# One matmul for the spread, mask first, values together, a shorter first selection and an earlier projection in a two-block kernel

## The reference

```python
score = sum_h w[t,h] * relu(qi[t,h] . ki[s] / sqrt(32))         # index score, masked to s <= t
idx = top_k(score, 256)
p = softmax(q . k[idx] / 8 + bias); o = p @ v[idx]              # DSA
p = softmax(q . k / 8 + c[t] - c[s], s <= t); o = p @ v         # FOX, c = cumsum log f
out = (o * silu(z)) @ w_out
```

## Time and profile before

| what | value |
|---|---|
| median of 3 runs | 3086.24 us (3084.36 to 3088.47) |
| profiled execution | 3079.65 us |
| its span | 3077.8 us, 40092 instructions |
| TensorE busy | 2876.6 us, 93% |
| VectorE busy | 1143.6 us, 37% |
| ScalarE busy | 895.2 us, 29% |
| GpSimd busy | 1031.6 us, 34% |

### The profile page before, as it was taken

One profiled execution on the slowest core, in us unless ns is written; L12 is line 12 of the kernel. 1 busy time (PEld: TensorE's weight loads), 2 busy tenths in 40 slices (PEclk: granted clock), 3 DMA queues, 4 the chain that ended last, 5 costly groups with the idle time before them and its releaser, 6 DMA issues.

```text
span 3077.8 us, 40092 instructions
## 1 busy us (share of the span) xinstructions
PE 2876.6 (93%) x16604; PEld 2199.7 (71%) x16604; DVE 1143.6 (37%) x2460; ACT 895.2 (29%) x1689; POOL 1031.6 (34%) x447
## 2 busy tenths in 40 slices
PE   6979977989899999999999999999999999998998
PEld 4746665668666666666787778787777878786886
DVE  7999987456522222223334201111111111114322
ACT  4412312452333333334212222222222222223112
POOL 2522273124322222123543333333333333333541
PEclk8979989999999999999999999999999999999999
DMA  4100011031111111112112111111111111113211
GB/s 102 35 21 21 21 53 54 29 111 42 42 48 42 49 49 42 48 49 76 55 59 78 41 42 42 42 42 42 39 45 35 48 42 42 42 42 131 62 48 62
DMA packets 222369, 155.05 MB, mean 50 GB/s; under 512 B 26294, under 2 KB 209116, under 8 KB 222060
## 3 DMA queue, kind: packets, MB, share of 16 engines
q1 hardware_dynamic: 210220, 122.62, 13.8%
q10 hardware_dynamic: 11968, 29.87, 2.7%
HBM read 132.99 MB, written 19.47 MB: 50 GB/s over the span
## 4 chain that ended last, share of the span: by engine, by line
PE 82%; DVE 8%; issue 3%; ACT 3%; POOL 2%; DMA 1%; ACTq 0%; DVEq 0%; POOLq 0%
PE proj L883 21%; PE proj L885 20%; PE proj L884 20%; PE score L1158 3%; PE out L1193 3%; PE score L1178 3%; DVE arena L2202 2%; DVE arena L2200 2%; PE score L1311 1%; PE out L1364 1%; PE out L1369 1%; PE out L1204 1%; PE score L1341 1%; PE out L883 1%; PE out L885 1%
## 5 line engine op out<-in xcount | busy, mean ns | idle before, releaser
L883 PE MATMUL proj<-act_hi,w_hi 128*128 128x512 f32 x2592 | 1056.7, 408 | 51.7 <-POOL w_lo L758 25.2
L756 POOL TENSOR_TENSOR w_hi<-w_raw,ones 128x1024 fp32r<-128x1024 f32 x181 | 431.7, 2385 | 1794.1 <-PE proj L885 1774.2
L884 PE MATMUL proj<-act_lo,w_hi 128*128 128x512 f32 x2592 | 1023.0, 395 | 0.0
L885 PE MATMUL proj<-act_hi,w_lo 128*128 128x512 f32 x2592 | 1022.8, 395 | 0.0
L883 PEld LDWEIGHTS proj<-act_hi,w_hi 128*128 128x128 f32 x2592 | 495.4, 191 | 185.2 <-issue 43.0
L885 PEld LDWEIGHTS proj<-act_hi,w_lo 128*128 128x128 f32 x2592 | 494.2, 191 | 107.8
L884 PEld LDWEIGHTS proj<-act_lo,w_hi 128*128 128x128 f32 x2592 | 495.9, 191 | 97.0 <-issue 0.2
L758 POOL TENSOR_TENSOR w_lo<-w_raw,w_hi 128x1024 fp32r<-128x1024 f32 x181 | 447.5, 2472 | 14.2
L1764 ACT ACTIVATE arena<-proj 128x512 f32<-128x512 f32 x236 | 174.9, 751 | 722.2 <-PE proj L885 696.5
L2340 DVE SCALAR_TENSOR_TENSOR arena<-arena,score 128x256 f32<-128x256 f32 (+1 forms) x192 | 76.9, 428 | 771.4 <-PE score L1311 726.2
L2240 DVE CUSTOM_DVE_ANT_0 arena<-arena,score 128x512 f32<-128x512 f32 (+2 forms) x192 | 102.8, 572 | 426.5 <-PE score L1164 285.1
(11 more groups left out here) (245 smaller groups left out, 2793.1 us busy)
## 6 DMA issues: line engine op xcount, KB each, us to landing
w_raw<-dil_w_in_dram SPq DMA_DIRECT2D x80, 512.0 KB, 3.7
w_raw<-fox_w_in_dram SPq DMA_DIRECT2D x32, 512.0 KB, 4.0
w_raw<-w_in_dram SPq DMA_DIRECT2D x23, 512.0 KB, 3.8
y_scratch<-arena ACTq DMA_DIRECT2D x21, 512.0 KB, 3.6
act_lo<-y_scratch SPq DMA_DIRECT2D x21, 512.0 KB, 6.3
arena<-decay_scratch ACTq DMA_DIRECT2D x16, 512.0 KB, 6.5
w_raw<-ple_w_gate_dram SPq DMA_DIRECT2D x16, 512.0 KB, 3.9
arena<-x_dram SPq DMA_DIRECT2D x12, 512.0 KB, 5.1
```

The source lines that it names most:

```text
L756: pool.tensor_tensor(hi, raw, one.unsqueeze(1).broadcast_to([P, KB, P]), ALU.mult).then_inc(w_hi_done, 1)
L883: pe.matmul(bank, hi, a_hi, start=first, stop=False)
L884: pe.matmul(bank, hi, a_lo, start=False, stop=False)
L885: return pe.matmul(bank, lo, a_hi, start=False, stop=last)
```

## The change

It has five parts.

- **Selection.** Tile 2 has 384 keys. Its scores are made with the opposite sign and, for the last 128 keys, with the mask subtracted; 16 rounds remove the 128 lowest in a reversed view of the row, and the mask is made with the opposite comparison. The index scores of tiles 3, 4 and 5 come earlier in the streams of TensorE, ScalarE and GpSimd, and TensorE waits for all of tile 5's ReLUs ahead of GLA. The pieces beside the rounds are placed anew: log gates, gate sums and decayed queries in tile 3, chunk keys in tile 4, chunk updates from round 17 of tile 4 to round 20 of tile 6, all gated outputs in tile 7.
- **GpSimd's gate products** stand ahead of weight tiles 19 and 20 instead of 18 and 19.
- **Projection of pair 2.** Its q and k (four half passes) are projected ahead of the second pooling product; pair 0's attention then carries two half passes in odd steps (v transposed) and pair 1's two (gate), with the turnings in steps 0 and 3.
- **Spread and mask.** VectorE copies the two inverses into a tile of 2 x 64 columns, with a wait for its own reciprocal, and TensorE spreads by one full-width matmul. The causal mask's matmuls come ahead of the scores and open the accumulation.
- **Values.** Both chunks' values stand behind the second chunk's transposes and the second part of the projection.

```diff
-IDX_STEPS = {0: (5, 1), 1: (5, 2), 2: (5, 3), 4: (6, 0), 5: (6, 1), 6: (6, 2), 7: (6, 3),
+IDX_STEPS = {4: (6, 0), 5: (6, 1), 6: (6, 2), 7: (6, 3),
...
-GLA_ROUNDS = {4: range(12, 32, 3), 5: range(0, 32, 2), 6: range(0, 18, 2)}
-TURNED_AT = {(6, 30): 0, (6, 31): 1, (7, 3): 2, (7, 5): 3, (7, 7): 4, (7, 9): 5}
+GLA_ROUNDS = {4: range(17, 32, 3), 5: range(0, 32, 2), 6: range(0, 22, 2)}
+TURNED_AT = {(7, 0): 0, (7, 1): 1, (7, 2): 2, (7, 4): 3, (7, 5): 4, (7, 8): 5}
...
-    if p == 0:
-        return [], unit(t // 2, t % 2), None, []
-    n = 4 + t // 2 if t < 4 else 6 + t // 2
-    return ([unit(7)] if t == 4 else []), unit(n, t % 2), None, ([unit(6)] if t == 3 else [])
+    n = (4 if p == 0 else 8) + t // 4
+    turned = [unit(6 + t // 3)] if p == 1 and t in (0, 3) else []
+    return turned, (unit(n, t // 2 % 2) if t % 2 else None), None, []
...
-            between = {5: (bias_negative, lambda: heads(3, 0)), 6: (lambda: heads(3, 2),), 7: (to_chunk_end,), 8: (lambda: heads(4, 0),),
-                       9: (decayed_keys, lambda: heads(4, 2)), 11: (lambda: heads(5, 0), lambda: heads(5, 2)),
+            between = {3: (lambda: heads(3, 0), lambda: heads(3, 2)), 5: (bias_negative,), 6: (lambda: heads(4, 0),),
+                       7: (lambda: heads(4, 2), to_chunk_end), 9: (decayed_keys,), 11: (lambda: heads(5, 0), lambda: heads(5, 2)),
...
-                       18: (lambda: gates((0, 1, 2)),), 19: (lambda: gates((3, 4)),), 21: (first_windows,),
+                       19: (lambda: gates((0, 1, 2)),), 20: (lambda: gates((3, 4)),), 21: (first_windows,),
...
+                        masked = causal(i, lo, w)
+                        if masked:
+                            for hh in range(2):
+                                end = hh * 512 + w
+                                pe.matmul(score[:, 0, end - P:end], diag_half[:, 0], diag_half[:, 1], start=True, stop=False,
+                                          skip_group_check=True)
...
-                        for hh in range(2):
-                            cols = slice(64 * hh, 64 * hh + 64)
-                            at = 32 + 2 * i + hh
-                            mm = pe.matmul(obanks[i % 2][cols, 256:384], R["st"][:, at:at + 1].broadcast_to([P, 64]),
-                                           ident[:, :], start=True, stop=True)
-                        mm.then_inc(S["bc"], 1)
+                        pe.matmul(obanks[i % 2][:, 256:384], R["o"][:, i % 2], ident[:, :],
+                                  start=True, stop=True).then_inc(S["bc"], 1)
...
                         scores(i + 1, 1)
-                        values(i, 0)
                         transposes(i, 1)
...
+                        values(i, 0)
                         values(i, 1)
...
                     project(1, halves[4:])
+                    project(2, halves[0:4])
                     pool_products(1)
...
-                pieces = {(2, 10): lambda: indexer_weights(obanks[0], 4, NT, 3), (2, 18): log_gates, (2, 22): gate_sums, (3, 3): decayed_queries, (3, 20): chunk_keys,
-                          (6, 20): inverse_roots, (7, 17): lambda: pool_outputs(0), (7, 26): lambda: pool_outputs(1)}
+                pieces = {(2, 14): lambda: indexer_weights(obanks[0], 4, NT, 3), (3, 7): log_gates, (3, 10): gate_sums, (3, 18): decayed_queries,
+                          (4, 8): chunk_keys, (6, 25): inverse_roots, (7, 18): lambda: pool_outputs(0), (7, 28): lambda: pool_outputs(1)}
...
-                for r in range(TOPK // 8):
+                row = scores[:, 0:w] if i > 2 else scores[:, 0:w][:, ::-1]
+                for r in range((TOPK if i > 2 else w - TOPK) // 8):
...
-                    dve.match_replace(scores[:, 0:w], top8, scores[:, 0:w], -3e38).then_inc(IX["top"], 1)
+                    dve.match_replace(row, top8, row, -3e38).then_inc(IX["top"], 1)
...
-                        dve.reciprocal(R["st"][:, 32 + 2 * i:34 + 2 * i], R["st"][:, 16 + 2 * i:18 + 2 * i]).then_inc(S["rden"], 1)
+                        inv = R["st"][:, 32 + 2 * i:34 + 2 * i]
+                        dve.reciprocal(inv, R["st"][:, 16 + 2 * i:18 + 2 * i]).then_inc(S["inv"], 1)
+                        wait_pass(dve, S["inv"], before + p, NT, i + 1)
+                        dve.tensor_copy(R["o"][:, i % 2].rearrange("p (h c) -> p h c", h=2),
+                                        inv.unsqueeze(2).broadcast_to([P, 2, 64])).then_inc(S["rden"], 1)
```

More of the change, by code:

```diff
@@ L549, in build @@
         PL = [None, PLE, dict(PLE, before=dict(tr=2, ev=2, ph=2, pl=2, up=2 * KB, t=2 * KB, h=2 * KB, **{"in": 16}))]
-        PAIR = sems("pair", "gate sdone sread pre mx edone rden tdone te pv y ysent yhi ylo bc mix")
+        PAIR = sems("pair", "gate sdone sread pre mx edone inv rden tdone te pv y ysent yhi ylo bc mix")
         AT = dict(dsa=PAIR, fox=PAIR, dil=sems("dil", "gate sdone sread pre mx edone rden tdone te pv y ysent yhi ylo oev ot"))
@@ L986, in idx_scores @@
                 for h in which:
-                    wait(pe, IX["relu"], (i - 2) * IDX_H + h - (1 if i <= 4 else 0))
+                    wait(pe, IX["relu"], (i - 2) * IDX_H + h - (1 if i <= 5 else 0))
                     for c in range(0, (i + 1) * P, 512):
@@ L1158, in scores @@
                             mm = pe.matmul(score[:, 0, hh * 512:hh * 512 + w], Q["q"][0][rows, i * P:(i + 1) * P],
-                                           Q["k"][0][rows, lo:lo + w], start=True, stop=not causal(i, lo, w),
-                                           skip_group_check=causal(i, lo, w))
-                        if causal(i, lo, w):
-                            for hh in range(2):
-                                end = hh * 512 + w
-                                mm = pe.matmul(score[:, 0, end - P:end], diag_half[:, 0], diag_half[:, 1], start=False, stop=True,
-                                               skip_group_check=True)
+                                           Q["k"][0][rows, lo:lo + w], start=not masked, stop=True,
+                                           skip_group_check=masked)
                         mm.then_inc(S["sdone"], 1)
@@ L1229, in one @@
                         if follow:
-                            project(next_pair(kind, p), head + [first_part])
+                            project(next_pair(kind, p), head + ([] if first_part is None else [first_part]))
                         elif i == NT - 1:
@@ L1711, in _ @@
             values(10, 0)
+            idx_relu(5, 0, 1)
             evac(11, targets[11])
@@ L1892, in attention @@
                     projected(1, 1, halves[6:])
+                    act.wait_ge(GL["mmul"], 5)
+                    projected(2, 2, halves[0:4])
                     for b in range(2):
```

44 lines of the change are left out of this document (25 added, 19 removed).

## The result

The changed kernel took 3002.5 us (median of 4 runs, 3000.2 to 3007.6) against 3085.3 us (3081.1 to 3088.5): ratio 0.9735, 95% interval 0.9717 to 0.9752, so 82 us (77 to 87) less. Forecast were 3040 us, 46 us less, and a range that ended at 3021: direction right, size little more than half, and the result outside the range. The profiled execution took 3003.2 us, its span is 3001.4 us.

The account below looks back on a forecast made before the run. TensorE was taken to bound the kernel (82% of the chain), with VectorE's rounds filling the selection. 15.5 + 16 + 15 = 46.5 us less made the median 3040 us; 8 in 10 between 3021 and 3061.

Parts of the forecast that it names:

- Parts 1 to 3: Selection of tile 2, first GLA chunk, way from GLA to attention: the attention starts 15.5 us earlier, at 486.7 us.
- the logarithm's place: In the selection: ScalarE's logarithm is needed only 8 rounds into tile 3, at 89.7 us; VectorE's 3.9 us wait goes.
- Part 4: Thinner filling of pairs 0 and 1: each gives up 10.9 us, returns about 7.3; with pair 2's 1.5, 16 us.
- Part 5, the spread's term: Second block: one full-width product of 0.225 us replaces two halves in 0.37 us; 64 steps x 0.145 = 9.3 us.
- Part 5, the values' term: Second block: values behind the projection's second part cover waits for ScalarE's copy; 5.7 of 10.2 us go.
- Mask and copy: Pair loop: mask first gains 0 (bounds 3 us either way); VectorE's copy, about 0.3 us, 88 times, costs nothing.
- (c): Rival: filling comes back whole and VectorE's lead comes through, 24 + 22 + 18 = 64 us: 3022 us; chance 0.10.
- (a): Rival: the stage before the attention gives nothing, 31 us remain: 3055 us; chance 0.13.
- (b): Rival: the pair loop's edits don't do what they say, 31.5 us remain: 3055 us; chance 0.10.
- (d): Rival, slower: GpSimd's splits hold VectorE's copy and the spread waits, 51 us lost: 3091 us, up to 3140; chance 0.05.

Follow-up runs that it names:

- a_oldloop: The changed kernel without its three pair-loop edits (mask last, spread by two column halves, values between second scores and second transposes): 3046.5 us, ratio 0.9875 to the kernel before.
- b_three: The kernel before with all three pair-loop edits (spread, mask, values) but the old order of selection, GLA and projections: 3044.1 us, ratio 0.9862.
- b_spread: The kernel before with the spread edit alone, VectorE's copy and one full-width product in all 88 steps: 3063.8 us, ratio 0.9924.

## Why the prediction was right in direction and wrong in size

**Parts 1 to 3, right in the main.** Forecast 15.5 us, measured 13.1. Tile 2 closes at 77.1 us (forecast 77.5), VectorE waits 3.9 us at the first chunk (4.5), closes tile 6 at 377.8 (381.5), waits 20.8 us for the second pooling product ("over 10"). No wait of TensorE for GpSimd is left between 345 and 485 us. The attention starts at 489.0 instead of 486.7. That it came so near is in part luck, since two misses have opposite signs: TensorE left GLA at 349.6 us, 2.4 earlier than the forecast's 352, and then took 128.5 us to the second pooling product, 5.1 more than the forecast's 123.4. In that stretch its waits for ScalarE's copies grew from 4.6 us in three to 8.6 us in six; the sum had no such term. (The sum for the logarithm's place, 57 + 20 + 12, is 89.0 and not 89.7; the log gates began at 90.7 us.)

**Part 4, the step that failed most.** "I take 2.6 us each for steps 4 and 6, 0.8 for step 2, 0.5 for step 0": the cost of a step without filling was mis-sized. In its place a_oldloop showed that the pairs lose nothing in sum: 26.6 us came back where 21.8 were taken out. Steps 2 and 6 of pair 0 lost 0.1 us and nothing. Step 4, with the end of step 3, gained 3.1 us beyond its filling. Step 0, with the slow clock that it left to step 1, lost 2.2 us, more than forecast, so not every term was too dear. The prediction's own rows had it for steps 4 and 6: 9.1 us with filling and 5.8 without differ by 3.3 us, more than the filling. What it had left out is that the same step holds GpSimd's split, beside which VectorE's maxima took 1.72 and 2.56 us instead of 0.49. With the loop's edits the pairs return 31.3 us (forecast 14.6), the loop's own share being 5.5 us by b_three's pairs (61.6 + 64.2 against 131.3).

**Part 5, the spread's term.** "64 steps x 0.145": measured 0.3 us a step by the rows and 23 / 88 = 0.27 by the time. The price of the full-width product came from eight in 1.80 us, 0.225 each; it takes 0.15. And the term counted only the spread's own row, while the transposes ahead of it took another 0.1 us too long.

**Part 5, the values' term.** The wait was sized rightly: 5.7 us forecast, 0.7 us in each of eight first steps measured. What was left out is the 0.15 to 0.2 us that a group of small products costs each time it stands by itself, and that is most of the 22 us. It was there to be read: a first projection behind a group took 0.31 to 0.34 us to its successor, where 0.23 is usual.

**Mask and copy, right.** The mask is worth 0 (-3 to +5 us). The copy is covered: 88 of them between 227 and 1578 ns, and nobody waited for one:

```profile
L2279 DVE COPY arena<-arena x88: 227/229/1578, 492.4 to 1397.6; 128x128 f32<-128x128 f32 x88
```

**Rivals.** (c) "more" is what happened, by half of its mechanism: the filling came back whole, but VectorE's lead did not come through (13.1 us against its 24). Its sum of 64 us was too small all the same, since it had the same two terms of the loop in it. (a), (b) and (d) fell. (d)'s holding is there in nine copies, but its place, the spread's wait, never opened; holding cost time elsewhere, at the maxima of step 4, and that already before the change.

**The range** left the result out because the bounds of the loop's terms were built around those prices: 20 us was the most given to the second block, and 39 came.

## What to carry to other kernels

Price a small TensorE product by the distance from the instruction before it to the one behind it, not by its own row: entering, leaving and starting a group costs 0.1 to 0.15 us each beside 0.055 us a record here, and with 88 steps that is the size of the whole effect. Before you charge a loop for thinner filling, follow its waits back to the instruction that was late: here it was a VectorE instruction that took up to 2.56 us instead of 0.49 beside a GpSimd split that served the filling, and it went when the filling went. And when work moves from a stage bound by TensorE to another such stage, expect little from the move itself.

## What the runs showed that was not expected

Two products of 64 columns are dearer than one of 128 by 0.3 us: 0.2 us in their own place, and 0.1 us because their first load starts late. VectorE's copies are at times held: 9 of the changed kernel's 88 took 0.69 to 1.58 us where 0.23 is usual (the longest in b_spread took 2.18 us). Eight of the nine overlap a GpSimd split and end within 0.1 us of its end, and none of the 79 others overlaps a GpSimd instruction. That agrees with what the Trainium skill (SBUF — State Buffer, section Who interferes with whom) says of a VectorE copy in a two-port mode and a GpSimd instruction; no run here takes GpSimd away from the copies, so for them the cause is read from the coincidence. For the maxima of step 4 the runs with and without the split there show it. And taking 21.8 us of independent products out of two pairs returned 26.6 us.
